# Embedding-gate units spread over fifteen expert pairs, with two weight buffers instead of three until pair 16

## What is computed

```python
eidx, gw = route(x2, lw['w_router'], lw['router_bias'])
ffn = (swiglu(x2, lw['w_s_gate'], lw['w_s_up'], lw['w_s_down'])
       + routed_experts(x2, eidx, gw, lw['w_e_gate'], lw['w_e_up'], lw['w_e_down']))
ple = jax.nn.sigmoid(h @ lw['w_ple_gate']) * (p @ lw['w_ple_proj'])
h = layer_norm(DN_ALPHA * h + ffn.reshape(n, s, D_MODEL) + ple, lw['ln2_g'], lw['ln2_b'])
```

## Time and profile before

| | us |
|---|---|
| median of 3 runs | 1364.27 (1363.01 to 1366.27) |
| the profiled execution | 1364.62 |
| its span, first to last instruction | 1362.8 |
| TensorE matmul busy | 1252.1 (92%) |
| VectorE busy | 499.0 (37%) |
| ScalarE busy | 298.9 (22%) |
| GpSimd busy | 129.9 (10%) |

### The profile page before, as it was taken

The page is one execution under the profiler, slowest core; times in us unless marked ns, Lnnn a source line. Parts: engine busy times, 40 slices in busy tenths (PEclk is TensorE's granted clock), DMA queues, the critical chain, the costliest instruction groups (busy, mean ns, idle before and its releaser), DMA issues.

```text
span 1362.8 us, 23702 instructions
## 1 busy us (share of the span) xinstructions
PE 1252.1 (92%) x8911; PEld 1008.6 (74%) x8912; DVE 499.0 (37%) x1090; ACT 298.9 (22%) x547; POOL 129.9 (10%) x200
## 2 busy tenths in 40 slices
PE   6999997999999999999889899989998799999675
PEld 6988876999999999998867667656665466666422
DVE  3455672324444233576862222111111111111128
ACT  3344452212212222224001111111111111111100
POOL 0200000000000000004000111111221121112100
PEclk8999996999999999999899999999999999999968
DMA  8211210222222231433346988999999999999592
GB/s 259 78 52 63 59 36 19 74 94 76 79 92 64 93 98 66 170 104 139 124 197 260 415 318 329 419 421 421 420 419 412 416 414 411 414 408 416 208 376 110
DMA packets 98318, 308.08 MB, mean 226 GB/s; under 512 B 11370, under 2 KB 62402, under 8 KB 73092
## 3 DMA queue, kind: packets, MB, share of 16 engines
q1 hardware_dynamic: 84692, 275.20, 53.0%
q0 software_dynamic: 12480, 28.60, 5.4%
q10 hardware_dynamic: 1088, 3.47, 0.7%
HBM read 295.95 MB, written 26.94 MB: 237 GB/s over the span
## 4 chain that ended last, share of the span: by engine, by line
PE 53%; DMA 35%; DVE 8%; DVEq 1%; issue 1%; ACT 1%; SPq 0%; ACTq 0%; POOLq 0%
DMA w_exp<-in_w_e_down_dram 33%; PE proj L963 31%; PE proj L1124 4%; PE att L1256 3%; PE att L1312 2%; PE att L1133 2%; PE proj L1329 2%; PE proj L1353 2%; PE att L1056 1%; DMA pg_raw<-in_w_ple_gate_dram 1%; PE att L1018 1%; PE att L1124 1%; PE att L1069 1%; DMA part<-expert_rows 1%; PE att L1092 0%
## 5 line engine op out<-in xcount | busy, mean ns | idle before, releaser
L1312 PE MATMUL att<-w_exp,xt 128*64 128x256 f32 x2560 | 289.4, 383 | 23.2 <-issue 11.3
L1312 PEld LDWEIGHTS att<-w_exp,xt 128*64 128x64 f32 x2560 | 221.0, 138 | 100.1 <-issue 46.1
L963 PE MATMUL proj<-h_hi,w_hi 128*128 128x288 f32 x800 | 178.3, 305 | 4.8 <-DVE h_lo L1365 4.8
L963 PE MATMUL proj<-h_lo,w_hi 128*128 128x288 f32 x800 | 171.9, 297 | 0.0
L963 PE MATMUL proj<-h_hi,w_lo 128*128 128x288 f32 x800 | 171.8, 297 | 0.0
L1329 PE MATMUL proj<-w_exp,ht_e 128*64 128x512 f32 x640 | 149.2, 607 | 11.2 <-DMA w_exp<-in_w_e_down_dram 6.6
L963 PEld LDWEIGHTS proj<-h_hi,w_hi 128*128 128x128 f32 x800 | 128.4, 190 | 20.2 <-issue 15.2
L963 PEld LDWEIGHTS proj<-h_lo,w_hi 128*128 128x128 f32 x800 | 129.7, 190 | 0.0
L963 PEld LDWEIGHTS proj<-h_hi,w_lo 128*128 128x128 f32 x800 | 129.4, 190 | 0.0
L432 DVE TENSOR_TENSOR w_lo<-w_raw,w_hi 128x2048 fp32r<-128x2048 f32 x33 | 75.6, 2291 | 100.1 <-ACT w_hi L422 94.7
L1329 PEld LDWEIGHTS proj<-w_exp,ht_e 128*64 128x64 f32 x640 | 51.1, 139 | 81.8 <-issue 80.0
(11 more groups left out here) (338 smaller groups left out, 1744.8 us busy)
## 6 DMA issues: line engine op xcount, KB each, us to landing
w_exp<-in_w_e_gate_dram SPq DMA_DIRECT2D x64, 1024.0 KB, 17.1
w_exp<-in_w_e_up_dram SPq DMA_DIRECT2D x64, 1024.0 KB, 17.4
w_exp<-in_w_e_down_dram SPq DMA_DIRECT2D x64, 1024.0 KB, 17.2
w_raw<-in_w_in_dram SPq DMA_DIRECT2D x21, 1024.0 KB
part<-expert_rows SPq DMA_DIRECT2D x4, 3072.0 KB, 27.2
w_raw<-in_w_in_dram SPq DMA_DIRECT2D x8, 512.0 KB
w_raw<-in_w_attn_out_dram SPq DMA_DIRECT2D x8, 512.0 KB
w_raw<-in_w_conv_out_dram SPq DMA_DIRECT2D x4, 1024.0 KB
```

Source lines behind the costliest of these rows:

```text
L963: last = nc.tensor.matmul(proj[:, 2 * i + a, 0:HALF], lhs, x[:, c, a * HALF:(a + 1) * HALF], start=(c == 0 and n == 0), stop=(c == KC - 1 ...
L1312: last = nc.tensor.matmul(att[e * SLOT:(e + 1) * SLOT, m, 0:FF], xt[:, c, e * SLOT:(e + 1) * SLOT], weights[e][:, c, :], start=(c == 0), s ...
```

## The change

- `N_TWO = 16`: pairs 0 to 15 use buffers 0 and 1 in turn, pair 16 is the first in buffer 2, and the ring of three begins with pair 17.
- `UNITS_AT`: units 5 to 9 stand one each after pairs 0 to 4, unit 10 after pair 7, two each after pairs 8 and 9, unit 15 after pair 12, two each after pairs 13 and 14. After every unit TensorE waits for its sigmoid.
- `GATE_SPLIT_AT`: the gate weights of blocks 2 and 3 are loaded after the parts of pairs 6 and 11 and split after pairs 6 and 11 (before: split after pairs 1 and 3).
- The projected embedding of block 1 is copied by ScalarE out of buffer 1's place into `ppo_1`, and `ppo_added` is now raised by that copy and by VectorE's addition of block 0: two counts, both before or at the start of pair 0. The down parts of pair 1 wait for these.
- Pair 2 is loaded like every other pair (by `next_pair`, before: with waits of its own).

```diff
-BUF_OF = (0, 1, 0, 1, 0, 1, 0, 2)
-RING = (1, 0, 2)
+N_TWO = 16
+BUF_OF = (0, 1) * (N_TWO // 2) + (2,)
+RING = (0, 1, 2)
+UNITS_AT = {0: (5,), 1: (6,), 2: (7,), 3: (8,), 4: (9,), 7: (10,), 8: (11, 12), 9: (13, 14),
+            12: (15,), 13: (16, 17), 14: (18, 19)}
+GATE_SPLIT_AT = {6: 2, 11: 3}
...
+        ppo_1 = at("ppo_1", [P, NT, GW], F32, o_x + 27648)
...
-            done = sp.value_load(cum_pass[0:1, 0:1], min_val=1, max_val=MAXPASS - 1)
-            sp.wait_ge(gu_ready, done)
-            past(nc.sync, 4)
-            landed_and_load(2, range(4))
-            sp.wait_ge(ppo_added, 1)
+            sp.wait_ge(ppo_added, 2)
             landed_and_load(1, range(4, 6))
-            landed_and_load(2, range(4, 6))
-            sp.wait_ge(u_ready, 2 * NT)
-            load_gate(2)
-            for p in range(3, 7):
+            for p in range(2, N_TWO):
                 next_pair(p, BUF_OF[p], p - 2)
-                if p == 4:
-                    sp.wait_ge(u_ready, 3 * NT)
-                    load_gate(3)
+                if p in GATE_SPLIT_AT:
+                    j = GATE_SPLIT_AT[p]
+                    sp.wait_ge(u_ready, j * NT)
+                    load_gate(j)
             sp.wait_ge(u_ready, 4 * NT)
             sp.wait_ge(res_done, 1)
-            for n in range(6):
-                part_landed(7, n)
-                load_part(7, BUF_OF[7], n)
-            with sp.Fori(0, (NPE - 8) // 3) as it:
+            landed_and_load(N_TWO, range(6))
+            with sp.Fori(0, (NPE - 1 - N_TWO) // 3) as it:
                 for i in range(3):
-                    next_pair(it * 3 + (8 + i), RING[i], it * 3 + (5 + i))
+                    next_pair(it * 3 + (N_TWO + 1 + i), RING[i], it * 3 + (N_TWO - 2 + i))
...
             nc.scalar.activation(hs_hi[:, :, :], hs_f[:, :, :], ACT.Copy).then_inc(hs_hd, 1)
+            act.wait_ge(pp_read, 2 * NT)
+            nc.scalar.activation(ppo_1[:, 0:NT - 1, :], ppo[0][:, 0:NT - 1, GW:2 * GW], ACT.Copy)
+            nc.scalar.activation(ppo_1[0:NS, NT - 1, :], ppo[0][0:NS, NT - 1, GW:2 * GW], ACT.Copy).then_inc(ppo_added, 1)
...
-            for p in range(8):
+            for p in range(N_TWO + 1):
                 pair(p, BUF_OF[p])
-                if p in (0, 2, 4):
-                    for u in range((1 + p // 2) * NT, (2 + p // 2) * NT):
-                        gate_unit(u)
-                    pe.wait_ge(u_sig, (2 + p // 2) * NT)
+                for u in UNITS_AT.get(p, ()):
+                    gate_unit(u)
+                    pe.wait_ge(u_sig, u + 1)
```

More of the change, by code:

```diff
@@ L273, in ppo_of @@
             j, t = u // NT, u % NT
+            if j == 1:
+                return ppo_1[0:ntok(t), t, :]
             return ppo[j // 2][0:ntok(t), t, j % 2 * GW:(j % 2 + 1) * GW]
@@ L929, in passes @@
                     act.reg_add(odd, odd, 1)
-            for p in range(5):
+            for p in range(N_TWO):
                 passes(p)
-                if p in (1, 3):
-                    gate_hi(2 + p // 3)
-                if p in (0, 2, 4):
-                    for u in range((1 + p // 2) * NT, (2 + p // 2) * NT):
-                        gate_sigmoid(u)
+                if p in GATE_SPLIT_AT:
+                    gate_hi(GATE_SPLIT_AT[p])
+                for u in UNITS_AT.get(p, ()):
+                    gate_sigmoid(u)
             for i, g in enumerate((ln2_g, ln2_b)):
                 act.dma_start(g2b2[:, i, :], g[0].partition_broadcast(P)).then_inc(ld_ln2, 16)
-            with act.Fori(0, NPE - 5) as it:
-                passes(it + 5)
+            with act.Fori(0, NPE - N_TWO) as it:
+                passes(it + N_TWO)
             for n, t in enumerate(LAST_ORDER):
@@ L1334, in pair @@
                     pe.reg_add(count, count, 1)
-            for p in range(8):
+            for p in range(N_TWO + 1):
                 pair(p, BUF_OF[p])
-                if p in (0, 2, 4):
-                    for u in range((1 + p // 2) * NT, (2 + p // 2) * NT):
-                        gate_unit(u)
-                    pe.wait_ge(u_sig, (2 + p // 2) * NT)
-            with pe.Fori(0, (NPE - 8) // 3) as it:
+                for u in UNITS_AT.get(p, ()):
+                    gate_unit(u)
+                    pe.wait_ge(u_sig, u + 1)
+            with pe.Fori(0, (NPE - 1 - N_TWO) // 3) as it:
                 for i in range(3):
-                    pair(it * 3 + (8 + i), RING[i])
+                    pair(it * 3 + (N_TWO + 1 + i), RING[i])
             for n, t in enumerate(LAST_ORDER):
@@ L1836, in _ @@
                 r = res[0:ntok(t), t, 0:GW]
-                nc.vector.tensor_tensor(r, r, ppo_of(t), ALU.add)
+                last = nc.vector.tensor_tensor(r, r, ppo_of(t), ALU.add)
+            last.then_inc(ppo_added, 1)
             count, odd = (dve.alloc_register(n) for n in ("pass_count_v", "pass_odd_v"))
@@ L1871, in ple_add @@
                 return nc.vector.tensor_tensor(r, r, ppo_of(u), ALU.add)
-            for p in range(5):
+            for p in range(N_TWO):
                 passes(p)
[L1875 to L1881, removed]
+                if p in GATE_SPLIT_AT:
+                    gate_lo(GATE_SPLIT_AT[p])
+                for u in UNITS_AT.get(p, ()):
+                    last = ple_add(u)
             last.then_inc(res_done, 1)
-            with dve.Fori(0, NPE - 5) as it:
-                passes(it + 5)
+            with dve.Fori(0, NPE - N_TWO) as it:
+                passes(it + N_TWO)
             dve.wait_ge(ld_ln2, 32)
```

## The result

The changed kernel takes 1378.76 us in the median (1373.23 to 1380.45), the kernel before, run beside it, 1364.41 us: ratio 1.0097, 95% interval 1.0066 to 1.0129. It is slower by about 14 us; the forecast was 1377 us.

A forecast was written before the change was run, and what follows sets the result against it. The weight stream was taken to set the end from buffer 2's first load on. Pair 16 released at 1014.8 us puts the last landing 13.0 us later: 1364.62 + 13.0 = 1377.6, given as 1377 us, range 1369 to 1386.

The forecast's parts named there:

- The bound: From the first load into buffer 2 the weight stream sets the end; ahead of it TensorE and the free buffers do.
- Start: Before pair 0's first pass, the larger ScalarE copies, some 1.5 us, vanish in ScalarE's 27.07 us of idle time.
- TensorE up to pair 15: Passes 234.2 us, lone units 54.2, second units 16.0, less 0.4: pair 15 starts 304.0 us after pair 0, at 1014.9 us.
- No wait for weights: Ahead of pair 15 down parts have 21 us to land and need 17.1 in the median, 22.9 at worst: no wait.
- rival A: Two buffers starve TensorE around the double pairs, delaying pair 16: about +6 us more, 1383 us; chance 0.12.
- Release: Unit 19 ends just ahead of pair 15, so SP issues pair 16 into buffer 2 at about 1014.8 us.
- The rest: After pair 16's issue, 38.7 us to pair 17's landing plus 243.9 to the last: 1297.4 us, 13.0 us later.
- The price of 2.0 us for a pass: In the weight stream, tokens gathered and scattered cost 66 / 33 = 2.0 us for each pass.
- Operand: Pair 1's down parts go out at about 714 instead of 739.27 us, filling the 730 us hole; gain only for the stream.
- The signs: Pair 16 issued near 1015 us, one-unit pairs 17.3 us apart, about 1.6 us idle behind units, last landing near 1297 us.
- B: Rival: lone units ahead of pair 15 cost less; 1368 us with half gone, 1364 with no change (chance 0.05).
- C: Rival: weights keep flowing without a hold and TensorE becomes the bound, 14.4 us less, 1350 us; 0.08 with any other gain.

The follow-up runs named there:

- changed again: The changed kernel measured once more, as it is, beside the last experiment on the same chip: 1380.16 us, ratio 1.0095.
- e1: The changed kernel with each pair's last unit result in a PSUM bank the next pass leaves alone, so no sigmoid wait behind it: 1362.56 us, ratio 0.9975.
- e2: The kernel before with TensorE waiting for the sigmoid after every unit of its blocks of five, 12 more waits: 1376.30 us, ratio 1.008.
- e3: The kernel before with only the buffers changed, two until pair 16, units still in blocks of five: 1368.01 us, ratio 1.0013.
- e4: The kernel before with block 1's operand moved to `ppo_1` and pair 2 loaded by `next_pair`: 1362.50 us, ratio 0.9981.
- e6: The same early units as e5, also on e1, but two buffers until pair 16: 1354.97 us, ratio 0.9928.
- e5: e1 with units placed earlier, the last five after pair 8, and the third buffer from pair 10 on: 1354.56 us, ratio 0.9928.
- e7: e1 with units 15 and 16 after pair 12, 17 to 19 after pair 13, none after pair 14: 1341.92 us, ratio 0.9831.

## Why the prediction was right

- *The bound.* The stream of weights sets the end from the release on, in every kernel with a hole ahead of it: changed, changed again and e1 lie 18 us apart in the release and take 284.5, 284.9 and 284.3 us from it. Shown.
- *Start.* From ScalarE's copy to `hs_hi` to the first pass it takes 29.44 us before (710.89 - 681.45) and 29.40 now (706.22 - 676.82): the copy to `ppo_1` costs nothing, as forecast.
- *TensorE up to pair 15.* 302.15 us measured, 304.0 forecast. A lone unit 4.93 by the rows of before, 4.92 measured. Second units 3.54 instead of 4.0 (four of them, 1.9 us): this was the term without a row, and the wake-up of some 0.5 us in it was too large. In e2 the sigmoid ends at 728.28 us (727.90 + 0.38) and the next unit's first matmul starts at 728.33, so the whole wait costs 0.72 us. The remainder agrees to 0.1 us, small differences cancelling; among them is pair 11, whose passes take 12.71 and 12.44 us instead of 12.33, the first with a wait of 0.37 us for VectorE's activation.
- *No wait for weights* (rival A). Right: no pass ahead of pair 15 waits for a landing in the timeline, and e3 gives two buffers 0 to 4 us.
- *Release.* SP issues at +302.05 us (forecast +303.9, from 1014.8 - 710.9).
- *The rest.* From the release to pair 17's landing 40.7 us (1030.45 + 18.54 = 1048.99; forecast 38.7), from there to the last landing at 1292.62 us 243.6 us (forecast 243.9). These 2 us too few and the 1.9 too many of TensorE cancel. That the sum came out at 13.0 against 12.9 us is luck to that extent: its parts were right to 2 us each. The price of 2.0 us for a pass rests on a miscount, 33 passes behind the release where pair 4's second pass belongs ahead of it and 32 are left; it makes 2.06 us and changes nothing.
- *Operand.* "A true gain for the stream, but only for the stream" was half right: in the old order (e4) it also brings the release forward by 5 us.
- *The signs.* SP's issue, the pitch of the pairs, the idle time behind each unit and the last landing came as said. "DMA share near 1 only after 1015 us" did not: the share is 1.01 already at 730 us and near 1 in most stretches, with pauses at the pairs with two passes, and the hole ahead of pair 16 is 28 us long (980 to 1008) where some 35 were expected. The sum did not use it: what the stream gains ahead of `res_done` it loses in waiting there.
- *The Trainium skill's figures.* By the Trainium skill's rule on the register load ("DMA: Bandwidth & Descriptors", Latency and other measured facts: at least about 600 ns) I worked out a sum 7 us lower, an estimate. The runs side with the row: the tail of a lone unit is 17.25 - 15.54 = 1.7 us, a wait without the load 0.72 us (e2), so load and refill together come to about 1.0 us. That is an estimate from these rows, since no run has the load by itself; it does not contradict a floor of 0.6 us. By the Trainium skill's rule of double buffering ("Trainium Kernel Development and Optimization", Best Practices) two buffers should do: e3 agrees (0 to 4 us), e6 against e5 only on balance, with some 9 us of pauses at pairs 10 and 11. It is no argument for the change, though, since what starved the stream was a lock on the third buffer that the queue reached too soon, and not the number of buffers.
- *Rivals B and C.* B's cheaper unit did not come. Its line, a gain once pair 15 starts 13 us earlier, fits e1: there it starts 19.4 us earlier, and the median is below that of the kernel before (ratio 0.9975). C's gain did not come either, but e7 shows that it was within reach: 1341.92 us, below the 1350 us that I had worked out for it, since e7 also drops the tails.

The profiled execution alone (1373.23 us) would have made the change look 5 us cheaper than it is.

## What to carry to other kernels

When a serial queue holds a transfer until the last piece of side work is done, look at the place of that last piece first: place it so that the queue is still busy when it ends (here ahead of the pair with two passes, one line worth 20 us). Even spreading comes after it, and is worth something too: 13 us between e6 and e7. Count the release of the lock by the work of the engine ahead of it, and the end by what the stream then has left. A wait for another engine directly ahead of a register load costs more than the same wait between matmuls (1.7 against 0.7 us here); give the result a bank of its own and the wait goes.

## What the runs showed of the hardware

The first half, the same in all kernels up to two copies, varied by 7 us between the profiled executions (first pass at 706.22 to 713.46 us). The chain of the changed kernel's two profiled executions shows where: the same 1536 matmuls,

```profile
228.57 202.31 PE proj L964 x1536
```

in the first, and in the repeated run:

```profile
228.35 207.73 PE proj L964 x1536
```

They start within 0.2 us of each other, and one takes 5.4 us longer. A stretch that lies inside both (PE, PEld, DVE, ACT, POOL busy, then PEclk, DMA share, GB/s), in the first and in the repeated run:

```profile
240.00:430.00 190.00, 190.00 (x1464) 190.00 (x1463) 76.42 (x123) 41.52 (x33) 0.00 (x0) 1.00 0.25 80
240.00:430.00 190.00, 190.00 (x1427) 190.00 (x1426) 73.67 (x120) 40.81 (x32) 0.00 (x0) 1.00 0.25 78
```

In both TensorE is busy without a gap and the granted clock is 1.00, but the matmuls start 0.130 us apart in one and 0.133 us in the other (190 / 1464 and 190 / 1427). Over 1536 of them that is about 5 us of the 5.4. Of the twelve profiled executions two have the quicker pace, this one and that of e5 (202.39 us), each the fastest execution of its kernel; the ten others took 206.57 to 207.73 us for the group. What sets the pace stays open.

The granted clock moves too, but gives little of it. TensorE waits 4.4 us for VectorE at about 210 us and then runs small matmuls with waits; the clock falls to its lower level (1.2 of 2.4 GHz, PEclk 0.50), in the first run with a short return at 214 us, and stands at it in both when the group begins. It is back at 1.00 by 236 us in both, in the first run 0.3 us of work sooner. Its mean over 200 to 240 us (0.74 against 0.66 in the repeated run) does not tell the quick executions from the others: e2, e4, e6 and e7 have 0.74 as well, with 207.25 to 207.34 us for the group. So a difference of a few us is better read from a common event inside the profile than from one execution's total.
